# GpSimd normalises the attention probabilities; the transposed tile stays one PSUM tile

## The chip, the core and the metric

One core of one Trainium2 chip. The metric is the device time of one execution in microseconds (us), taken as the median of several runs. Two layers of a hybrid transformer backbone run as one program.

## The reference, cut to what matters

The change lies in attention, which each layer computes once for the 512 latent tokens (768 keys), and layer 0 also for the 256 context tokens (256 keys). There are 8 query heads of 64 channels on 2 key/value heads.

```python
def attention(q, k, v):
    ...
    def one_block(qi):
        s = jnp.einsum('bqhgd,bshd->bhgqs', qi, k).astype(jnp.float32)
        p = jax.nn.softmax(s, axis=-1).astype(v.dtype)
        return jnp.einsum('bhgqs,bshd->bqhgd', p, v)
    ...

def reference(...):
    for i in range(DEPTH):
        last = i == DEPTH - 1
        ...
        yx = mixer_out(qx, k_all, v_all, ux[..., V_END:P_END], ux[..., P_END:C_END], ux[..., C_END:], lp)
        if not last:
            yc = mixer_out(qc, kc, vc, uc[..., V_END:P_END], uc[..., P_END:C_END], uc[..., C_END:], lp)
        ...
```

## The kernel before

The program is written by hand, one instruction list for each engine; each list runs in order, and semaphores order the lists against one another. A counter (`Tally`) gives every awaited step a name; `seen(name)` is the semaphore value that a waiter needs.

Float32 products are made of three reduced-precision ones, so every operand exists as a high and a low part. Weights come in slabs of 128x1024: the SP queue loads a slab, ScalarE rounds it to the high part (L893), and GpSimd subtracts to get the low part (`split_run`, L425), two instructions ahead in a ring of four. These splits are GpSimd's main work.

Attention is cut into **units** (`units`, L274). A unit is one query tile of 128 rows against 768 keys; in layer 0 each head has a fifth, short unit that packs the two context query tiles against 256 keys each, a tile of 128x512. Layer 0 has 40 units, layer 1 has 32. All engines walk over the units in a software pipeline; the order is written out by hand in each list:

- TensorE (L765): scores of unit u+1 into PSUM region A (two buffers), then the six transposes of unit u-1 into PSUM region B (L736; one buffer), then a share of the products with the values (L757).
- VectorE (L1580): maximum of unit u (L1585) and its negative, scaled (L1589); for unit u-1 the reciprocal of the row sums (L1596) and the **normalisation**, the probabilities times that reciprocal in place (L1599); for unit u-2 the low part of the transposed tile, read from B (L1605). The last one frees B.
- ScalarE (L1067): exponential of unit u with its row sums (L1075), which frees A; then the high part of the transposed tile of unit u-1, read from B (L1086).

The transposes of a unit wait for its normalisation (`normed`) and for B to be free (`free`, `pt`). The probabilities have two buffers (`pr`, `probs` in the profile), and the exponential of unit u waits for the transposes of unit u-2.

GpSimd has no part in attention. Its list (L480) goes from the splits ahead of attention straight on to those behind it. The slabs of a layer are numbered; S_CONV is 8, RING is 4, so slab 12 is the last that GpSimd splits before attention ends: ScalarE rounds slab 13 only behind its own attention loop, at `result_of(s0 + S_CONV + 2)` (L1100).

Of the kernel before, what the change touches and what calls it, by code (L numbers as in the profile page):

```python
# [28 lines left out]
ALU = mybir.AluOpType  # L29
# [19 lines left out]
RING = 4  # L49
# [11 lines left out]
SLABS = _s  # L61
# [59 lines left out]
def build(nc, io, known):  # L121
# [22 lines left out]
    def seen(*name):  # L144


        if name not in known:
            assert not known, name
            return tallies["rounded"].sem, 1
        tally, value = known[name]  # L150
        return tallies[tally].sem, value
# [3 lines left out]
    with ctx:  # L155
# [107 lines left out]
        def lo_of(ly):  # L263

            return 0 if ly == 0 else CTX
# [8 lines left out]
        def units(ly):  # L274


            out, b = [], 0
            for h in range(HEADS):
                for q0, nq, nk in ([(CTX, 2, T), (CTX + 2 * P, 2, T)] + ([(0, 1, CTX)] if ly == 0 else [])):
                    out += [(h, q0, nk, q, nq, b) for q in range(nq)]  # L280
                    b += 1
            return out
# [23 lines left out]
        def q_tiles(unit):  # L306

            return 2 if unit[2] == CTX else 1
# [109 lines left out]
        @block.gpsimd  # L418
        def _(pool):

            def split_run(a, b):
                for s in range(a, b):
                    n = P * (slab_blocks(s % SLABS) if s >= RING else KT)
                    pool.wait_ge(rounded.sem, s + 1)
                    nc.gpsimd.tensor_tensor(wl[:, s % RING, 0:n], raw[:, s % RAW, 0:n], wh[:, s % RING, 0:n],  # L425
                                            ALU.subtract).then_inc(split, 1)

            def add_squares(ly, st, lo, k):
                pool.wait_ge(*seen("sq", ly, st, k))
                pool.wait_ge(*seen("sq", ly, st, k - 1))  # L430
                nc.gpsimd.tensor_tensor(square(k - 1)[:, lo:T], square(k - 1)[:, lo:T], square(k)[:, lo:T],
                                        ALU.add).then_inc(*pool_norm.up("sq2", ly, st, k - 1))

            def x_times(ly, st, lo, j):

                x_old = xm if st == "post1" else x
                if st == "post1":
                    pool.wait_ge(x_loaded[j], 16 * (ly + 2))
                pool.wait_ge(*seen("gy", ly, st, j))
                if j >= 2:  # L440
                    pool.wait_ge(*seen("vadd", ly, st, j - 2))
                out = xgy[:, j % 2, lo:T] if j else xgy_sum[:, lo:T]
                nc.gpsimd.tensor_tensor(out, x_old[:, j, lo:T], acc[:, j, lo:T], ALU.mult).then_inc(
                    *pool_norm.up("xgy", ly, st, j))

            def add_x(ly, st, lo, k):

                pool.wait_ge(*seen("rt", ly, st, k))
                nc.gpsimd.tensor_tensor(x[:, k, lo:T], x[:, k, lo:T], acc[:, k, lo:T], ALU.add).then_inc(
                    *pool_norm.up("x", ly, st, k))  # L450

            def ff_lows():

                pool.wait_ge(*seen("stat", 0, "pre2"))
                pool.wait_ge(*seen("fh", "shift"))
                nc.gpsimd.tensor_tensor(fl[:, :, 0:2], mod[:, 0, 3 * KT:4 * KT, :], fh[:, :, 0:2],
                                        ALU.subtract).then_inc(*pool_norm.up("fl", "shift"))
                for k in range(KT):
                    pool.wait_ge(*seen("fh", k))
                    nc.gpsimd.tensor_tensor(fl[:, k, 2:2 + T], ns[:, k, :], fh[:, k, 2:2 + T],  # L460
                                            ALU.subtract).then_inc(*pool_norm.up("fl", k))

            def lows(ly, st, lo):

                for k in lows_of(ly, st):
                    t = norm_tile(k) if (ly, st) == (0, "pre1") else scaled_tile(k)
                    pool.wait_ge(*seen("hh", ly, st, k))
                    nc.gpsimd.tensor_tensor(hl[:, k, lo:T], t[:, lo:T], hh[:, k, lo:T],
                                            ALU.subtract).then_inc(*pool_norm.up("hl", ly, st, k))
                    if (ly, st) == (1, "pre1") and k in (0, 2):  # L470
                        add_x(0, "post2", 0, pool_adds[k // 2])


            split_run(0, 2)
            for k in range(1, KT, 2):
                add_squares(0, "pre1", 0, k)
            split_run(2, RING)
            lows(0, "pre1", 0)
            at_s = RING
            for ly in range(LAYERS):  # L480
                lo = lo_of(ly)
                for j in range(KT):
                    stop = ly * SLABS + S_OUT + j + RING
                    split_run(at_s, stop)
                    at_s = stop
                    if j < KT - 1:
                        x_times(ly, "post1", lo, j)
                if ly == 0:
                    ff_lows()
                else:  # L490
                    lows(1, "pre2", lo)
                if ly == 0:
                    for j in range(KT):
                        stop = FF_OUT[2] + j + RING
                        split_run(at_s, stop)
                        at_s = stop
                        if j < KT - 1:
                            x_times(ly, "post2", lo, j)
                    split_run(at_s, SLABS + RING)
                    at_s = SLABS + RING  # L500
                    lows(1, "pre1", 0)
                else:
                    split_run(at_s, LAYERS * SLABS)
                    for k in pool_last:
                        add_x(ly, "post2", lo, k)
# [780 lines left out]
        def _(dve):  # L1286
            v = nc.vector

            def link(ins, tally, *name):

                ins.then_inc(*tally.up(*name))
                dve.wait_ge(*tally.ago())
# [229 lines left out]
            for ly in range(LAYERS):  # L1522
# [57 lines left out]
                for u in range(len(us) + 2):  # L1580
# [11 lines left out]
                    if 1 <= u <= len(us):  # L1592
                        h, q0, nk, q, nq, b = us[u - 1]
                        n, c = q_tiles(us[u - 1]), 2 * ((u - 1) % 8)
                        dve.wait_ge(*seen("free", "scores", ly, u - 1))
                        link(v.reciprocal(ust[:, 3, c:c + n], ust[:, 2, c:c + n]), dve_tmp)  # L1596
                        for r in range(n):
                            p_r = pr[:, (u - 1) % 2, r * nk:(r + 1) * nk]
                            v.tensor_scalar(p_r, p_r, ust[:, 3, c + r:c + r + 1], None, ALU.mult).then_inc(  # L1599
                                *(dve_tmp.up("normed", ly, u - 1) if r == n - 1 else dve_tmp.up()))  # L1600
                    if u >= 2:
                        h, q0, nk, q, nq, b = us[u - 2]
                        dve.wait_ge(*seen("pth", ly, u - 2))
# [375 lines left out]
```

## Time and profile before

| | |
|---|---|
| median of 3 runs | 2241.17 us (2239.71 to 2244.13) |
| the profiled execution: time, span | 2242.06 us, 2240.3 us |
| busy, of the span | TensorE 95%, VectorE 60%, ScalarE 35%, GpSimd 35% |
| VectorE's multiplies (L1599) | 80, median 0.62 us each |
| attention, from the first maximum to the last subtraction | 157.7 to 272.7 us (layer 0), 1426.2 to 1518.8 us (layer 1) |

The profile is one execution. Its rows name the engine (PE is TensorE, PEld its weight loads, DVE is VectorE, ACT is ScalarE, POOL is GpSimd), the line of the kernel, what is written and what is read, and, in brackets, how long the engine had stood idle and which instruction ended that. The first instruction with such a bracket is where a wait ended. Matmuls are pipelined, so a group's time runs from its first start to its last end.

### The profile page before, as it was taken

Reading aid. Unit: us, or ns where it says so; the run is one execution under the profiler, and the core shown is the slowest. Engines: PE = TensorE matmul, PEld = TensorE weight load, DVE = VectorE, ACT = ScalarE, POOL = GpSimd, SP = SyncE. Lnnn points to the kernel's source line nnn. Section 1 sums busy time; section 2 is a strip of 40 time slices with the busy share of each in tenths; the row PEclk is TensorE's granted clock in tenths of the full one; section 3 lists DMA queues with packets and bytes.
Section 4 is the critical chain, followed back from the end, with each engine's and each line's share of the span. In section 5 each row is a group of like instructions: output and inputs, shape, how many; then the busy total and the mean of one; then the engine's idle time right before and its main releaser. Section 6 shows DMA issues by size and latency. Waiting matters only on the chain.

```text
span 2240.3 us, 27947 instructions
## 1 busy us (share of the span) xinstructions
PE 2134.7 (95%) x11302; PEld 1807.4 (81%) x11302; DVE 1337.7 (60%) x1812; ACT 794.9 (35%) x1154; POOL 783.3 (35%) x359
## 2 busy tenths in 40 slices
PE   6889899999999999999999987899999999999997
PEld 6777788888888888888888876677867877888885
DVE  6459899856774587847616674798954353101113
ACT  2446711142324522223212344572234344222223
POOL 3220023232334433423323345103444555444442
PEclk9999999999999999999999989999999999999998
DMA  7110012123344134534323221102222332323321
GB/s 295 38 47 1 1 52 70 43 88 112 105 159 151 58 119 134 187 101 135 105 85 111 94 95 66 48 1 66 88 78 90 108 123 82 97 94 95 94 85 66
DMA packets 63200, 205.24 MB, mean 92 GB/s; under 512 B 7136, under 2 KB 8288, under 8 KB 62816
## 3 DMA queue, kind: packets, MB, share of 16 engines
q1 hardware_dynamic: 57744, 190.87, 26.2%
q10 hardware_dynamic: 5328, 12.59, 1.5%
q8 instruction: 90, 1.47, 0.3%
q14 instruction: 38, 0.31, 0.0%
HBM read 197.79 MB, written 5.64 MB: 91 GB/s over the span
## 4 chain that ended last, share of the span: by engine, by line
PE 78%; DVE 17%; ACT 2%; issue 1%; DMA 1%; POOL 1%; ACTq 0%; DVEq 0%
PE ps L529 70%; DVE conv_acc L1624 3%; DVE ps L1624 2%; DVE unit_stats L1585 2%; PE ps L555 2%; DVE pt1l L1605 1%; DVE probs L1599 1%; DVE pt0l L1605 1%; PE ps L736 1%; PE ps L592 1%; PE ps L573 1%; PE ps L613 1%; PE ps L583 1%; PE ps L757 1%; PE ps L600 1%
## 5 line engine op out<-in xcount | busy, mean ns | idle before, releaser
L425 POOL TENSOR_TENSOR w_l<-w_raw,w_h 128x1024 fp32r<-128x1024 f32 (+3 forms) x296 | 683.7, 2314 | 1305.7 <-ACT w_h L893 1305.4
L529 PE MATMUL ps<-h_h,w_h 128*128 128x512 f32 (+1 forms) x1296 | 430.4, 372 | 5.9 <-ACT t L1145 4.2
L529 PE MATMUL ps<-h_l,w_h 128*128 128x512 f32 (+1 forms) x1296 | 426.1, 369 | 0.0
L529 PE MATMUL ps<-h_h,w_l 128*128 128x512 f32 (+1 forms) x1296 | 425.3, 368 | 0.0
L893 ACT ACTIVATE w_h<-w_raw 128x1024 fp32r<-128x1024 f32 (+3 forms) x296 | 280.5, 950 | 212.2 <-PE ps L529 148.6
L529 PEld LDWEIGHTS ps<-h_h,w_h 128*128 128x128 f32 x1296 | 244.8, 190 | 55.8 <-ACT t L1145 6.6
L529 PEld LDWEIGHTS ps<-h_h,w_l 128*128 128x128 f32 x1296 | 245.7, 190 | 43.6
L529 PEld LDWEIGHTS ps<-h_l,w_h 128*128 128x128 f32 x1296 | 245.4, 189 | 42.9 <-issue 1.2
L1485 DVE CUSTOM_DVE_ANT_0 ps<-ada_raw,c_row 128x1024 f32<-128x1024 f32 x160 | 268.4, 1677 | 9.1 <-DMA ada_raw<-in_ada 4.1
L529 PE MATMUL ps<-f_h,w_h 128*128 128x258 f32 (+1 forms) x672 | 173.1, 339 | 0.9 <-DVE t L1810 0.9
L529 PE MATMUL ps<-f_h,w_l 128*128 128x258 f32 (+1 forms) x672 | 173.5, 340 | 0.0
L529 PE MATMUL ps<-f_l,w_h 128*128 128x258 f32 (+1 forms) x672 | 172.4, 338 | 0.0
L529 PE MATMUL ps<-mid_h,w_l 128*128 128x512 f32 (+1 forms) x528 | 160.7, 359 | 0.0
L529 PE MATMUL ps<-mid_h,w_h 128*128 128x512 f32 (+1 forms) x528 | 160.0, 357 | 0.1
L529 PE MATMUL ps<-mid_l,w_h 128*128 128x512 f32 (+1 forms) x528 | 159.1, 355 | 0.0
L1624 DVE SCALAR_TENSOR_TENSOR ps<-conv_in,vec,ps 128x512 f32<-128x512 f32 (+1 forms) x180 | 143.8, 845 | 2.1
L529 PEld LDWEIGHTS ps<-f_h,w_h 128*128 128x128 f32 x672 | 127.5, 190 | 16.1 <-DVE t L1810 1.2
L529 PEld LDWEIGHTS ps<-f_l,w_h 128*128 128x128 f32 x672 | 127.1, 189 | 14.6
L529 PEld LDWEIGHTS ps<-f_h,w_l 128*128 128x128 f32 x672 | 127.0, 189 | 14.6
L529 PEld LDWEIGHTS ps<-mid_h,w_h 128*128 128x128 f32 x528 | 99.4, 188 | 16.2 <-DVE acc L1835 0.4
L529 PEld LDWEIGHTS ps<-mid_l,w_h 128*128 128x128 f32 x528 | 99.2, 188 | 15.5
L529 PEld LDWEIGHTS ps<-mid_h,w_l 128*128 128x128 f32 x528 | 99.2, 188 | 14.7
(236 smaller groups left out, 3222.6 us busy)
## 6 DMA issues: line engine op xcount, KB each, us to landing
w_raw<-in_w SPq DMA_DIRECT2D x222, 512.0 KB, 3.6
ada_raw<-in_ada SPq DMA_DIRECT2D x80, 512.0 KB, 3.6
w_raw<-in_w SPq DMA_DIRECT2D x50, 256.0 KB, 3.2
ada_first<-in_ada SPq DMA_DIRECT2D x16, 512.0 KB, 6.7
w_raw<-in_w SPq DMA_DIRECT2D x16, 384.0 KB, 3.1
x<-in_x ACTq DMA_DIRECT2D x8, 384.0 KB, 17.6
x_again<-in_x ACTq DMA_DIRECT2D x8, 384.0 KB, 7.7
x_between<-x SPq DMA_DIRECT2D x8, 384.0 KB, 2.3
```

The costliest lines, as they stand in the source:

```text
L425: nc.gpsimd.tensor_tensor(wl[:, s % RING, 0:n], raw[:, s % RAW, 0:n], wh[:, s % RING, 0:n], ALU.subtract).then_inc(split, 1)
L529: ins = nc.tensor.matmul(at(out, c0, c1), w[:, s % RING, b * P:(b + 1) * P], m[:, kt, first + c0:first + c1], start=(kt == 0 and n == 0), ...
L555: ins = nc.tensor.matmul(at(out, c0, c1), w[:, s % RING, b * P:(b + 1) * P], m[:, k, first + c0:first + c1], start=(i == 0 and n == 0), st ...
L573: ins = nc.tensor.matmul(DD[:, 2 * k:2 * k + 2], ada_first[:, n % ADA_SLOTS, b * P:(b + 1) * P], silu_c[:, b, :], start=(b == 0), stop=(b ...
L583: ins = nc.tensor.matmul(at(B if w == "B" else OD, c0, c1), mat, src(c0, c1), start=True, stop=True)
L592: ins = nc.tensor.matmul(token_sum(kind, TOK[kind] + t, 1), src[:, t * P:(t + 1) * P], ones[:, 0:1], start=start and first, stop=stop and ...
L600: ins = nc.tensor.matmul(token_sum("q", c, 2), src[:, t * P:(t + 1) * P], blk[:, 0:P:HD], start=True, stop=True)
L893: nc.scalar.activation(wh[:, n % RING, 0:nb * P], raw[:, n % RAW, 0:nb * P], ACT.Copy).then_inc(*rounded.up())
L1485: link(v.tensor_tensor_reduce(out=scratch, in0=tile, in1=c_row[:, s, :], scale=1.0, scalar=0.0, op0=ALU.mult, op1=ALU.add, accum_out=mod[: ...
L1585: link(v.reduce_max(ust[:, 0, c:c + n], at(A[u % 2], 0, n * nk).rearrange("p (r k) -> p r k", k=nk), AX.X), dve_tmp)
L1605: v.tensor_tensor(key_rows(pl, us[u - 2]), by_key_tile(at(B, 0, nk * q_tiles(us[u - 2])), us[u - 2]), key_rows(ph, us[u - 2]), ALU.subtrac ...
L1624: return v.scalar_tensor_tensor(out=taps_of(ly, j), in0=src, scalar=w, in1=taps_of(ly, j), op0=ALU.mult, op1=ALU.add)
```

## The change

For each unit VectorE keeps the reciprocal and signals it (`recip`). The multiply by it, in place in the same buffer, goes to GpSimd, in a new loop `probabilities`. It waits for `recip` of the unit and signals `normed` from a counter of GpSimd. Ahead of that loop stands a `split_run` up to slab 12, so that the multiplies of a layer lie between the split of slab 12 and that of slab 13. The transposed tile is one piece in B as before, with one transpose group, one high and one low part for each unit. TensorE's and ScalarE's lists are as before.

```diff
@@ -471,6 +471,16 @@
+            def probabilities(ly):
+
+                for u, (h, q0, nk, q, nq, b) in enumerate(units(ly)):
+                    n, c = q_tiles((h, q0, nk, q, nq, b)), 2 * (u % 8)
+                    pool.wait_ge(*seen("recip", ly, u))
+                    for r in range(n):
+                        p_r = pr[:, u % 2, r * nk:(r + 1) * nk]
+                        nc.gpsimd.tensor_scalar(p_r, p_r, ust[:, 3, c + r:c + r + 1], None, ALU.mult).then_inc(
+                            *(pool_norm.up("normed", ly, u) if r == n - 1 else pool_norm.up()))
@@ -479,6 +489,9 @@
             for ly in range(LAYERS):
                 lo = lo_of(ly)
+                split_run(at_s, ly * SLABS + S_CONV + 1 + RING)
+                at_s = ly * SLABS + S_CONV + 1 + RING
+                probabilities(ly)
                 for j in range(KT):
@@ -1593,11 +1606,7 @@
                         dve.wait_ge(*seen("free", "scores", ly, u - 1))
-                        link(v.reciprocal(ust[:, 3, c:c + n], ust[:, 2, c:c + n]), dve_tmp)
-                        for r in range(n):
-                            p_r = pr[:, (u - 1) % 2, r * nk:(r + 1) * nk]
-                            v.tensor_scalar(p_r, p_r, ust[:, 3, c + r:c + r + 1], None, ALU.mult).then_inc(
-                                *(dve_tmp.up("normed", ly, u - 1) if r == n - 1 else dve_tmp.up()))
+                        v.reciprocal(ust[:, 3, c:c + n], ust[:, 2, c:c + n]).then_inc(*dve_tmp.up("recip", ly, u - 1))
```

VectorE, inside a head of layer 0, before: from the subtraction of a long unit over the maximum of the short unit (128x2) to the next subtraction but one.

```order
L1605 TENSOR_TENSOR pt0l<-ps,pt0h 128x6x128 [waits act_hi]
L1585 TENSOR_REDUCE unit_stats<-ps 128x2 [waits pe_done]
L1589 SCALAR_TENSOR_TENSOR unit_stats<-unit_stats,token_rs 128x2 [waits dve_tmp]
L1596 RECIPROCAL unit_stats<-unit_stats 128x1 [waits act_out]
L1599 TENSOR_SCALAR probs<-probs,unit_stats 128x768 [waits dve_tmp]
L1605 TENSOR_TENSOR pt0l<-ps,pt0h 128x6x128 [waits act_hi]
L1585 TENSOR_REDUCE unit_stats<-ps 128x1 [waits pe_done]
L1589 SCALAR_TENSOR_TENSOR unit_stats<-unit_stats,token_rs 128x1 [waits dve_tmp]
L1596 RECIPROCAL unit_stats<-unit_stats 128x2 [waits act_out]
L1599 TENSOR_SCALAR probs<-probs,unit_stats 128x256 [waits dve_tmp]
L1599 TENSOR_SCALAR probs<-probs,unit_stats 128x256
L1605 TENSOR_TENSOR pt0l<-ps,pt0h 128x6x128 [waits act_hi]
```

The same place after the change; its lines are numbered 9 or 13 higher.

```order
L1614 TENSOR_TENSOR pt0l<-ps,pt0h 128x6x128 [waits act_hi]
L1598 TENSOR_REDUCE unit_stats<-ps 128x2 [waits pe_done]
L1602 SCALAR_TENSOR_TENSOR unit_stats<-unit_stats,token_rs 128x2 [waits dve_tmp]
L1609 RECIPROCAL unit_stats<-unit_stats 128x1 [waits act_out]
L1614 TENSOR_TENSOR pt0l<-ps,pt0h 128x6x128 [waits act_hi]
L1598 TENSOR_REDUCE unit_stats<-ps 128x1 [waits pe_done]
L1602 SCALAR_TENSOR_TENSOR unit_stats<-unit_stats,token_rs 128x1 [waits dve_tmp]
L1609 RECIPROCAL unit_stats<-unit_stats 128x2 [waits act_out]
L1614 TENSOR_TENSOR pt0l<-ps,pt0h 128x6x128 [waits act_hi]
```

The multiplies and their wait on the reciprocal are gone; the subtraction follows the reciprocal directly.

GpSimd, around the start of attention in layer 0, before.

```order
L468 TENSOR_TENSOR h_l<-norm_tmp,h_h 128x768 [waits act_hi] x3
L425 TENSOR_TENSOR w_l<-w_raw,w_h 128x1024 [waits rounded] x13
L425 TENSOR_TENSOR w_l<-w_raw,w_h 128x512 [waits rounded]
L425 TENSOR_TENSOR w_l<-w_raw,w_h 128x1024 [waits rounded]
L425 TENSOR_TENSOR w_l<-w_raw,w_h 128x512 [waits rounded]
```

And after (one head of the eight; the other seven repeat the last three rows).

```order
L468 TENSOR_TENSOR h_l<-norm_tmp,h_h 128x768 [waits act_hi] x3
L425 TENSOR_TENSOR w_l<-w_raw,w_h 128x1024 [waits rounded] x9
L481 TENSOR_SCALAR probs<-probs,unit_stats 128x768 [waits dve_tmp] x4
L481 TENSOR_SCALAR probs<-probs,unit_stats 128x256 [waits dve_tmp]
L481 TENSOR_SCALAR probs<-probs,unit_stats 128x256
```

Of the 13 splits in a row nine now stand ahead of the multiplies and four behind them.

## Rows read from the trace of the kernel before

**Rows 1.** The page's chain of waits, shares of the span by engine.

```profile
PE 78%; DVE 17%; ACT 2%; issue 1%; DMA 1%; POOL 1%; ACTq 0%; DVEq 0%
```

**Rows 2.** Windows: span; busy us (count) of PE, PEld, DVE, ACT, POOL; clock; DMA.

```profile
182.76:264.15 81.39, 74.15 (x542) 62.53 (x541) 76.97 (x157) 59.65 (x121) 0.00 (x0) 1.00 0.01 1
1443.00:1506.73 63.73, 60.59 (x439) 50.63 (x438) 62.11 (x116) 45.49 (x82) 0.00 (x0) 1.00 0.00 1
```

**Rows 3.** Timeline, layer 1: start us, us, engine, line, operation, out<-in, count, [idle before <-releaser].

```profile
1443.00 0.96 DVE L1605 TENSOR_TENSOR pt1l<-ps,pt1h 128x768 fp32r<-128x768 f32 x1
...
1443.93 0.96 DVE L1585 TENSOR_REDUCE unit_stats<-ps 128x1 f32<-128x768 f32 x1
...
1444.01 0.64 PEld L736 LDWEIGHTS ps<-const,probs 128*128 128x128 f32 x6 [0.56 <-DVE pt1l L1605]
...
1444.01 0.87 PE L736 MATMUL ps<-const,probs 128*128 128x128 f32 x6
...
1444.92 0.16 DVE L1589 SCALAR_TENSOR_TENSOR unit_stats<-unit_stats,token_rs 128x1 f32<-128x1 f32 x1
...
1444.92 0.81 ACT L1086 ACTIVATE pt1h<-ps 128x768 fp32r<-128x768 f32 x1 [0.73 <-PE ps L736]
...
1445.00 0.16 DVE L1596 RECIPROCAL unit_stats<-unit_stats 128x1 f32<-128x1 f32 x1
...
1445.19 0.62 DVE L1599 TENSOR_SCALAR probs<-probs,unit_stats 128x768 f32<-128x768 f32 x1
...
1445.77 0.96 DVE L1605 TENSOR_TENSOR pt1l<-ps,pt1h 128x768 fp32r<-128x768 f32 x1
...
1445.79 0.87 PE L726 MATMUL ps<-k_split,q_split 128*128 128x256 f32 x4
...
1446.69 0.96 DVE L1585 TENSOR_REDUCE unit_stats<-ps 128x1 f32<-128x768 f32 x1
```

**Rows 4.** Timeline, layer 0, around the short unit of a head.

```profile
188.31 0.96 DVE L1605 TENSOR_TENSOR pt0l<-ps,pt0h 128x768 fp32r<-128x768 f32 x1
...
189.32 0.66 PE L736 MATMUL ps<-const,probs 128*128 128x128 f32 x4 [0.15 <-DVE pt0l L1605]
...
190.01 0.60 ACT L1086 ACTIVATE pt0h<-ps 128x512 fp32r<-128x512 f32 x1 [0.77 <-PE ps L736]
...
190.46 0.62 DVE L1599 TENSOR_SCALAR probs<-probs,unit_stats 128x768 f32<-128x768 f32 x1
...
191.00 0.68 DVE L1605 TENSOR_TENSOR pt0l<-ps,pt0h 128x512 fp32r<-128x512 f32 x1
...
193.57 0.95 DVE L1605 TENSOR_TENSOR pt1l<-ps,pt1h 128x768 fp32r<-128x768 f32 x1
```

**Rows 5.** Timeline, the first unit of each layer's attention loop.

```profile
161.25 0.16 DVE L1596 RECIPROCAL unit_stats<-unit_stats 128x1 f32<-128x1 f32 x1 [0.17 <-ACT probs L1075]
...
162.30 0.22 PEld L736 LDWEIGHTS ps<-const,probs 128*128 128x128 f32 x1
...
1429.10 0.17 DVE L1596 RECIPROCAL unit_stats<-unit_stats 128x1 f32<-128x1 f32 x1 [0.17 <-ACT probs L1075]
...
1430.07 0.85 PE L736 MATMUL ps<-const,probs 128*128 128x128 f32 x6
```

**Rows 6.** GpSimd's two-input instruction: timeline, and mean by form (last row).

```profile
1348.86 0.94 DVE L1371 TENSOR_TENSOR acc<-acc,ps 128x768 f32<-128x768 f32 x1
...
1349.88 1.83 POOL L449 TENSOR_TENSOR x<-x,acc 128x768 f32<-128x768 f32 x1 [0.28 <-DVE acc L1371]
...
L449 POOL TENSOR_TENSOR x<-x,acc 128x512 f32<-128x512 f32 x4 | 5.1, 1264 | 23.1 <-DVE acc L1371 23.1
```

**Rows 7.** Timeline, layer 0, VectorE beside a running GpSimd instruction.

```profile
157.65 2.36 POOL L425 TENSOR_TENSOR w_l<-w_raw,w_h 128x1024 fp32r<-128x1024 f32 x1 [0.73 <-ACT w_h L893]
...
157.68 0.96 DVE L1585 TENSOR_REDUCE unit_stats<-ps 128x1 f32<-128x768 f32 x1
...
158.67 1.35 DVE L1589 SCALAR_TENSOR_TENSOR unit_stats<-unit_stats,token_rs 128x1 f32<-128x1 f32 x1
```

## Prediction

> **What bounds the kernel now.** I read the page's chain of waits first: TensorE is 78% of it, VectorE 17% [rows 1], so a VectorE instruction is worth something only where TensorE waits for VectorE. The change touches one stage, attention, which the kernel passes twice: 40 units in layer 0, 32 in layer 1. The windows over its steady part come next [rows 2]. The granted clock is 1.00 (2.4 GHz). Layer 1: 116 VectorE instructions at five a unit are 23 units in 63.73 us, **2.77 us a unit**. Layer 0: six heads, from the first subtraction of one to that of the sixth after it, take 81.39 us, 13.57 us for a head's five units. GpSimd does nothing there. TensorE (60.59 us busy) and VectorE (62.11) look equally full, so busy time does not name the bound; the order of events does.
>
> The timeline of one unit says what 2.77 us is made of [rows 3]. PSUM region B holds one transposed tile. VectorE subtracts it (L1605, starting 1443.00, 0.96); 0.05 later TensorE transposes the next (1444.01, 0.87, after an idle 0.56 that the subtraction ended); 0.04 later ScalarE copies it (1444.92, 0.81); 0.04 later VectorE subtracts again (1445.77). 0.96 + 0.05 + 0.87 + 0.04 + 0.81 + 0.04 = 2.77 us. I call it the B ring. It closes exactly on the measured period, and **the normalisation is not in it**. VectorE's own sequence is nearly as long: the normalisation runs from 1445.19 to 1445.81 and overlaps the start of the next subtraction, with some 0.05 us to spare. Two limits lie on top of each other; taking work from one leaves the other.
>
> In layer 0 the fifth unit of a head is short (two query tiles of 256 keys, a 128x512 tile). Its ring is shorter, and there VectorE is the later one [rows 4]: the copy of the short tile ends at 190.61, but the subtraction starts at 191.00, behind the normalisation that began at 190.46. From 188.31 over 191.00 to 193.57 the two steps take 5.26 us. The ring alone would need 0.96 + 0.05 + 0.66 + 0.03 + 0.60 + 0.03 = 2.33 for the step to the short tile, and 0.68 + 0.05 + 0.87 + 0.04 + 0.81 + 0.04 = 2.49 for the step back: 4.82.
>
> **What the change removes.** The multiplies on VectorE: one of 0.62 us for each long unit [rows 3], two half-size ones for a short unit, 72 slots of 0.54 us because the next instruction overlaps (190.46 to 191.00, [rows 4]). In layer 1 the freed time is worth nothing: the B ring still takes 2.77. In layer 0 at most 5.26 - 4.82 = 0.44 us for each of the 7 places where a short unit stands between two long ones: 3.1 us in all. That is the ceiling of the gain, 0.14% of the span.
>
> **What it adds.** The same multiplies on GpSimd, X us for a long unit, and two handovers. VectorE to GpSimd took 0.08 (1348.86 + 0.94 to 1349.88, [rows 6]); GpSimd to TensorE I take as the same, so 0.15 for both. No GpSimd multiply by a scalar is in this trace. From below X is bounded by VectorE's 0.62 for the same tile. From above by GpSimd's two-input instruction on a tile of this size, 1.83 [rows 6]. A gain from X below 0.62 would change nothing, since the ring is then the later one in any case. Between the ends: 512 elements took 1.26 and 768 took 1.83, so 2.2 ns an element and 0.15 fixed. The two-input form moves three streams, the multiply two; two thirds of 1.68 plus 0.15 is 1.27. I take **X = 1.3**, an estimate, and keep both ends. A short unit's two multiplies of 256 elements come by the same reckoning to 2 x (0.15 + 0.37) = 1.04, less than X, and are nowhere the later ones.
>
> **The wait that it adds.** Transpose of unit u+2 now follows this path from transpose of unit u, through program order on TensorE and VectorE: transposes and values until the next scores start (1444.01 to 1445.79, 1.78), scores 0.87 and handover 0.03 (reduction starts 1446.69), the reduction to the reciprocal 1.07 (0.99 + 0.08), the reciprocal 0.16, 0.15 handovers and X [rows 3, 4]. That is 4.06 + X for two units, against 5.54 from two turns of the B ring. **The break-even is X = 1.48.** Below it, layer 1 keeps its 2.77. At the short unit of layer 0 the ring gives 4.82, so there the path rules from X = 0.76 on: 4.06 + 1.3 = 5.36, 0.10 more than today's 5.26; break-even 1.20.
>
> In front of each loop nothing hides the multiply, since the first transpose waits for it. Layer 1: reciprocal at 1429.10 + 0.17 + 0.15 + 1.3 = 1430.72, where the transpose began at 1430.07: 0.6 late. Layer 0: 161.25 + 0.16 + 0.15 + 1.3 = 162.86 against a weight load at 162.30: 0.6 late [rows 5]. X enters these two places in full. At the end of each loop the last units run on the ring, and nothing changes.
>
> GpSimd's queue: the weight splits of slabs up to 12 stand ahead of the multiplies, the split of slab 13 behind all of them. ScalarE rounds slab 13 only after attention, so no split comes later; GpSimd is idle in between [rows 2], and X of 1.3 to 1.83 fits in 2.77. SP's queue is not touched. Cost: nothing.
>
> **A port.** VectorE's tiny negmax at 158.67 took 1.35 us instead of 0.16, and ended with the GpSimd instruction that had started at 157.65 and took 2.36; the reduction before it, which reads PSUM, ran its usual 0.96 under the same instruction [rows 7]. So here a GpSimd instruction held up a VectorE one with two SBUF inputs, and spared one that reads PSUM, as the subtraction also does with one of its inputs. In the new loop one such instruction per unit remains, the negmax. It starts 0.08 before the reciprocal that releases the multiply, so the multiply has 2.77 - 0.08 - 0.16 - 0.08 = 2.45 us until the next negmax. It collides only from X = 2.45.
>
> **The sum.** Layer 0: 7 x 0.10 = 0.7, its start 0.6. Layer 1: 0 and 0.6. Together +1.9 us on the profiled execution's own 2242.06 us: 2244.0. That execution lies 0.9 above the median of the runs, so on the scale of the medians **2243 us**.
>
> **Rivals.**
> A, *slower: GpSimd becomes the late one.* Mechanism and place as above, deciding from X = 1.48 on in both layers. At X = 1.83: layer 1 pays (4.06 + 1.83 - 5.54) = 0.35 for two units, 15.5 times: 5.4. Layer 0's head becomes 5.89 + 5.89 + 2.77 = 14.55 instead of 13.57, seven times: 6.9. The two starts: 2 x (0.6 + 0.53) = 2.3. Sum +14.6: 2256.7, or 2256 by the medians. The 4.5 us that count as slower are reached at X = 1.51 (3.5 us at 1.48, and some 31 us for each us of X beyond). For it: every large GpSimd row is a two-input one at 1.83. Against: the multiply reads one stream less. The Trainium skill (GPSIMD Engine Reference, Performance versus the Vector engine) speaks for a middle: it measures some 1.8 cycles an element for a tight loop, an estimate of 1.15 us for 768 elements at its 1.2 GHz, and the sum by it would be 2242; for the two-input form it gives about 2.6 cycles, which the trace's 2.2 ns an element bears out.
> B, *GpSimd runs at VectorE's pace.* X = 0.62: 7 x -0.44 = -3.1, starts -0.2: -3.3, 2238.8, or 2238 by the medians, which still counts as no change. The Trainium skill (GPSIMD Engine Reference, Engine selection) calls a one-input elementwise operation "roughly line-rate" on GpSimd; by that this rival is the result. No row here shows a one-input form, so I give it a fair chance and not the most.
> C, *faster: VectorE is the bound in attention.* For it: 17% of the chain of waits is VectorE's [rows 1], and it is busy 62.11 of 63.73 us [rows 2]. Were it so, each unit would lose its 0.54 slot: 72 x 0.54 = 39 us, 2203. Against it stands the ring, which closes to 0.01 us with a wait of TensorE on the subtraction in every unit.
> D, *it does not do what it says.* The order of the instructions shows the multiplies gone from VectorE and standing on GpSimd, so this is excluded.
>
> **How the numbers follow.** The forecast case, X from 0.9 to 1.5, gets 0.46; B, X below 0.9, 0.18; A 0.31; C and anything that gains beyond the ceiling 0.05. A difference of 0.2% (4.5 us) is about the least that a measurement of this kernel can tell from no change. B and the forecast case both stay inside it: same 0.64, slower 0.31, faster 0.05. The range goes from rival B's end to just beyond A's at X = 1.83: 2237.5 to 2257.
>
> **What the new profile would show.** The GpSimd rows of the multiply give X directly; everything else follows from it. Right: the subtractions of layer 1 still 2.77 apart, VectorE idle some 0.5 a unit, the transposes still waiting for the subtraction; in layer 0 a head at 13.1 to 13.7. Wrong: transposes released by GpSimd in layer 1 (X over 1.48, rival A), a negmax longer than 0.16 inside the loop, a period under 2.77 (rival C), or a second stretch of lower clock behind the later start of layer 0, which this sum holds at nothing.

## The result, and the profile after

The changed kernel takes 2271.97 us (median of four runs, 2270.04 to 2275.16) against 2240.44 for the kernel before on the same chip (four runs, 2239.43 to 2244.13). The ratio is 1.0139, with a 95% interval of 1.0122 to 1.0157: slower by 31.5 us, where 2243 was forecast and 2257 was the end of the range. The profiled execution spans 2269.0 us, 28.7 more than the one before.

The page's first section, and its chain of waits by engine (the line that answers [rows 1]):

```profile
PE 2134.7 (94%) x11302; PEld 1807.8 (80%) x11302; DVE 1299.2 (57%) x1732; ACT 795.1 (35%) x1154; POOL 940.7 (41%) x439
...
PE 76%; DVE 14%; POOL 4%; ACT 3%; issue 2%; DMA 1%; ACTq 0%; DVEq 0%; SPq 0%
```

GpSimd now holds 4% of the chain, where it had 1%. VectorE fell from 60% busy to 57%, and that bought nothing. The groups of GpSimd's new line, long and short units apart (busy, mean ns of one | idle time before and what ended it):

```profile
L481 POOL TENSOR_SCALAR probs<-probs,unit_stats 128x768 f32<-128x768 f32 x64 | 141.2, 2207 | 60.0 <-DVE unit_stats L1609 60.0
L481 POOL TENSOR_SCALAR probs<-probs,unit_stats 128x256 f32<-128x256 f32 x16 | 14.6, 927 | 12.7 <-DVE unit_stats L1609 12.7
```

**The multiply takes 2.21 us.** The prediction took 1.3, between 0.62 and 1.83. It is slower than the two-input instruction of the same size [rows 6], which was to be its upper bound. All 64 take between 2.20 and 2.21, whatever VectorE does beside them, so no collision with VectorE makes them long.

The same two windows as [rows 2], with the same columns:

```profile
182.76:264.15 81.39, 63.69 (x470) 53.99 (x468) 53.22 (x107) 52.44 (x106) 56.52 (x32) 1.00 0.00 1
1443.00:1506.73 63.73, 52.40 (x343) 44.20 (x343) 39.88 (x77) 36.51 (x64) 43.09 (x20) 0.89 0.01 3
```

In layer 1's window TensorE issues 343 matmuls where it issued 439, and in layer 0's 470 where it issued 542. The list of waits of 180 to 280 (us in total, times, longest) says on whom it waits, with GpSimd in turn waiting for the reciprocal:

```profile
POOL probs L481 <- DVE unit_stats L1609: 31.5, 34, 1.6
PE ps L749 <- POOL probs L481: 20.4, 27, 1.5
```

And the timeline of layer 1, the place that answers [rows 3], is one closed path over two units:

```profile
1488.96 2.21 POOL L481 TENSOR_SCALAR probs<-probs,unit_stats 128x768 f32<-128x768 f32 x1 [1.14 <-DVE unit_stats L1609]
...
1491.32 0.84 PE L749 MATMUL ps<-const,probs 128*128 128x128 f32 x6 [0.73 <-POOL probs L481]
...
1493.04 0.87 PE L739 MATMUL ps<-k_split,q_split 128*128 128x256 f32 x4
...
1493.94 0.96 DVE L1598 TENSOR_REDUCE unit_stats<-ps 128x1 f32<-128x768 f32 x1
...
1495.02 0.15 DVE L1609 RECIPROCAL unit_stats<-unit_stats 128x1 f32<-128x1 f32 x1
...
1495.26 2.21 POOL L481 TENSOR_SCALAR probs<-probs,unit_stats 128x768 f32<-128x768 f32 x1 [1.11 <-DVE unit_stats L1609]
```

The path runs so: the multiply of unit u (2.21), 0.15 to TensorE, transposes and values of unit u up to the scores of unit u+3 (1.72), their maximum starting 0.90 later, the reciprocal of unit u+2 1.08 after that (0.15), and 0.09 to GpSimd: 6.30 us, with the multiply of unit u+1 in between at 1491.94. The subtractions (L1614) stand 3.31 and 3.00 apart by turns, 6.31 for two units, where the B ring needed 5.54. The bracket behind the transposes names GpSimd, as the prediction said it would if X were over 1.48.

**Where the 28.7 us lie.** Layer 0's first subtraction comes 0.7 later than before, and its loop, from first to last subtraction, takes 120.55 us instead of 106.94 (+13.6). In layer 1 the first subtraction comes 7.91 us behind the first maximum instead of 5.74 (+2.2), and the loop takes 99.54 instead of 85.89 (+13.65). The stretch between the two loops is 1.6 shorter. Sum 28.5.

### The profile page after: what moved, and what is told of

It is laid out like the page before. It is cut to its first block, busy times and chain, and to the rows that moved or that the text cites. A ratio compares the mean times of both kernels' runs of the same rounds, so it can differ in the third digit from the quotient of the medians.

```text
span 2269.0 us, 27947 instructions
## 1 busy us (share of the span) xinstructions
PE 2134.7 (94%) x11302; PEld 1807.8 (80%) x11302; DVE 1299.2 (57%) x1732; ACT 795.1 (35%) x1154; POOL 940.7 (41%) x439
## 3 DMA queue, kind: packets, MB, share of 16 engines
q8 instruction: 90, 1.47, 0.3%
## 4 chain that ended last, share of the span: by engine, by line
PE 76%; DVE 14%; POOL 4%; ACT 3%; issue 2%; DMA 1%; ACTq 0%; DVEq 0%; SPq 0%
PE ps L542 69%; POOL probs L481 3%; DVE conv_acc L1633 3%; DVE ps L1633 2%; PE ps L749 2%; PE ps L568 2%; DVE unit_stats L1598 1%; PE ps L586 1%; DVE pt1l L1614 1%; PE ps L605 1%; ACT pt1h L1099 1%; DMA w_raw<-in_w 1%; PE ps L596 1%; DVE pt0l L1614 1%; PE ps L626 1%
## 5 line engine op out<-in xcount | busy, mean ns | idle before, releaser
L481 POOL TENSOR_SCALAR probs<-probs,unit_stats 128x768 f32<-128x768 f32 (+1 forms) x80 | 155.8, 1951 | 72.7 <-DVE unit_stats L1609 72.7
```

Source lines behind the costliest of these rows:

```text
L481: nc.gpsimd.tensor_scalar(p_r, p_r, ust[:, 3, c + r:c + r + 1], None, ALU.mult).then_inc(*(pool_norm.up("normed", ly, u) if r == n - 1 els ...
```

## The experiments

All ratios are to the kernel before on the same chip, with their 95% interval. X is GpSimd's time for one multiply of a long unit.

### Is it X? The same multiply over fewer columns

Two kernels are the changed one with the multiply cut to its first 8 columns, and to half of its columns.

```diff
-                        p_r = pr[:, u % 2, r * nk:(r + 1) * nk]
+                        p_r = pr[:, u % 2, r * nk:r * nk + 8]
```

> The changed kernel, but GpSimd multiplies only the first 8 columns of each tile (the rest stays unnormalised); both handovers and all waits stay. Theory (the length X of the multiply is the whole cost): X near 0.3 us, the B ring rules everywhere, subtractions of layer 1 2.77 us apart, a head of layer 0 at 13.1; about 4 us under the kernel before: 2236 to 2238. Rival (the handovers between engines, or GpSimd and VectorE blocking each other, make the cost): it stays at 2255 or more.

```diff
-                        p_r = pr[:, u % 2, r * nk:(r + 1) * nk]
+                        p_r = pr[:, u % 2, r * nk:r * nk + nk // 2]
```

> The changed kernel with the multiply on the first half of the columns (384 of 768; the rest stays unnormalised). From 0.93 us for 256 and 2.21 us for 768 columns X should be 1.25, under the break-even of 1.48: 2.77 a unit in layer 1, a head of 13.6 in layer 0, both starts 0.5 late: 2241 to 2243, no difference from the kernel before. If cost grows in proportion to the length instead of setting in at a break-even, half of the loss stays: 2256.

The groups of the multiply, of the first kernel and then of the second:

```profile
L481 POOL TENSOR_SCALAR probs<-probs,unit_stats 128x8 f32<-128x8 f32 x80 | 24.3, 306 | 172.7 <-DVE unit_stats L1609 172.7
```

```profile
L481 POOL TENSOR_SCALAR probs<-probs,unit_stats 128x384 f32<-128x384 f32 x64 | 79.6, 1244 | 95.8 <-DVE unit_stats L1609 95.8
```

Times: 2242.81 us at X = 0.31, ratio 0.9999 (0.9985 to 1.0013), and 2247.61 at X = 1.24, ratio 1.0018 (1.0003 to 1.0032). In both, layer 1's subtractions are 2.77 apart once the loop is under way: **X makes the lengthening of the steady loop**, and the new semaphores and handovers cost it nothing. The second time is a miss all the same: 2241 to 2243 was expected, no difference, and it is 4 us (1 to 7) slower. Its first units of layer 1 are late (see the clock, below). At X = 1.24 the two steps around a short unit of layer 0 take 2.34 + 3.02 = 5.36 us, where the path gives 4.06 + 1.24 = 5.30. At X = 0.31 they take 2.34 + 2.63 = 4.97, not the 4.82 that the prediction took as the ring's floor. That shrinks the possible gain, and the first kernel does not reach the 2236 to 2238 that I expected of it; its first units in both layers ran at 3.43 us instead of 2.77 (see the clock, below).

### What sets X? Other forms of the same instruction

The two-input form, which reads the reciprocal as a broadcast operand:

```diff
-                        nc.gpsimd.tensor_scalar(p_r, p_r, ust[:, 3, c + r:c + r + 1], None, ALU.mult).then_inc(
+                        nc.gpsimd.tensor_tensor(p_r, p_r, ust[:, 3, c + r:c + r + 1].to_broadcast([P, nk]), ALU.mult).then_inc(
```

> The multiply as a two-input GpSimd instruction, the reciprocal broadcast along the row by its access pattern. If the two-input form costs 1.83 us as it does elsewhere in this kernel, layer 1 takes (4.06 + 1.83) / 2 = 2.95 a unit and the time falls by 16 us to 2256. If the broadcast operand or this place in the loop makes any GpSimd instruction take 2.2, the time stays at 2272.

And the scalar form with a constant in place of the operand:

```diff
-                        nc.gpsimd.tensor_scalar(p_r, p_r, ust[:, 3, c + r:c + r + 1], None, ALU.mult).then_inc(
+                        nc.gpsimd.tensor_scalar(p_r, p_r, 0.5, None, ALU.mult).then_inc(
```

> The changed kernel with the constant 0.5 in place of the reciprocal as the multiplier (output not the reference's), to measure the instruction: if reading the per-row scalar is what makes it 2.21 us, it falls to 1.3 or below and the time to some 2243; if the loop over the elements is, it stays at 2.2 and the time at 2272.

The groups of the multiply, of the one and then of the other:

```profile
L481 POOL TENSOR_TENSOR probs<-probs,unit_stats 128x768 f32<-128x768 f32 x64 | 93.9, 1467 | 86.5 <-DVE unit_stats L1609 86.5
```

```profile
L481 POOL TENSOR_SCALAR probs<-probs 128x768 f32<-128x768 f32 x64 | 136.4, 2132 | 62.7 <-DVE unit_stats L1609 62.6
```

I had expected 1.83 of the two-input form, and it takes **1.47**. The kernel takes 2249.79 us, ratio 1.0035 (1.0021 to 1.0048), so naming another instruction gets back three quarters of the loss. It also lands on the predicted break-even: 4.06 + 1.47 = 5.53 against the ring's 5.54, and the subtractions of layer 1 are 2.78 apart. The prediction's sum at that X was some 3.5 us; measured are 8, and about 2 of the difference are three first units of layer 1 at 3.44, 3.44 and 3.57 us. The constant changes X only from 2.21 to 2.13 (2268.23 us in one run), so it is the scalar form that is slow here, not the reading of its operand. Why that form is slow, no run shows. The period follows: 4.06 + 2.13 = 6.19 for two units, and 3.11 measured for one.

### Does the wait path decide? The reciprocal ahead of the maximum

With X left at 2.21, the reciprocal of unit u-1 is put ahead of the maximum of unit u on VectorE. That takes the scores and the maximum out of the path.

```diff
                 for u in range(len(us) + 2):
+                    if 1 <= u <= len(us):
+                        ...
+                        dve.wait_ge(*seen("free", "scores", ly, u - 1))
+                        v.reciprocal(ust[:, 3, c:c + n], ust[:, 2, c:c + n]).then_inc(*dve_tmp.up("recip", ly, u - 1))
                     if u < len(us):
...
-                    if 1 <= u <= len(us):
-                        ...
-                        dve.wait_ge(*seen("free", "scores", ly, u - 1))
-                        v.reciprocal(ust[:, 3, c:c + n], ust[:, 2, c:c + n]).then_inc(*dve_tmp.up("recip", ly, u - 1))
```

> The changed kernel with one step moved: VectorE takes the reciprocal of unit u-1 ahead of the maximum of unit u, not behind it. The multiply still takes 2.21 us. Theory (what costs is the wait path, which runs through the maximum): the multiply starts some 0.9 us sooner, the path through three units becomes 7.6 us against 8.3 for the B ring, the ring rules again at 2.77 a unit: 2240 to 2245. Rival (a GpSimd multiply of 2.2 us is too long for the loop wherever it stands): 2265 or more.

2254.17 us, ratio 1.0042 (1.0026 to 1.0058): 22 of the 31 us are back with X unchanged. So the path through program order was the cause, and X its largest term. It still misses the 2240 to 2245 expected. In layer 1 most subtractions are 2.76 to 2.80 apart, but six are 3.07 or 3.08. There the transposes are released by GpSimd: ScalarE's copy of a finished product (L1076, 0.38 us at 1459.05) stands ahead of the exponential, and multiply and transposes (1463.17) come late by it. In this trace the six make some 2 us, three first units at 3.43, 3.43 and 3.64 another 2, and the later first subtraction of layer 1 makes 2.8.

The multiply now overlaps VectorE's negmax (L1607 here), which reads two SBUF inputs. First a long unit, where the negmax is not held up, then a short one, where it is:

```profile
1486.02 2.21 POOL L481 TENSOR_SCALAR probs<-probs,unit_stats 128x768 f32<-128x768 f32 x1 [0.16 <-DVE unit_stats L1598]
...
1486.81 0.16 DVE L1607 SCALAR_TENSOR_TENSOR unit_stats<-unit_stats,token_rs 128x1 f32<-128x1 f32 x1
```

```profile
183.49 2.20 POOL L481 TENSOR_SCALAR probs<-probs,unit_stats 128x768 f32<-128x768 f32 x1 [0.82 <-DVE unit_stats L1598]
...
184.01 0.39 DVE L1607 SCALAR_TENSOR_TENSOR unit_stats<-unit_stats,token_rs 128x2 f32<-128x2 f32 x1
```

What differs is how far the multiply has come. The 55 negmaxes that run beside a long multiply in this trace and start 0.79 us or more behind its start take 0.16. The eight that start 0.53 behind it take 0.38 or 0.39 and end 0.91 behind it, 1.3 us before the multiply does. So the scalar form holds VectorE up as well, but only early in its run and not to its end.

### Would VectorE's time have been worth anything? No multiply at all

The kernel before without its multiplies, on any engine: rival C's question.

```diff
-                        link(v.reciprocal(ust[:, 3, c:c + n], ust[:, 2, c:c + n]), dve_tmp)
-                        for r in range(n):
-                            ...
+                        v.reciprocal(ust[:, 3, c:c + n], ust[:, 2, c:c + n]).then_inc(*dve_tmp.up("normed", ly, u - 1))
```

> The kernel before without any normalising multiply (output not the reference's); the transposes wait for the reciprocal only. It prices the freed VectorE time. B ring: layer 1 still 2.77 a unit, a head of layer 0 at 13.3, 2236 to 2239. If VectorE is the bound in attention: 0.54 for each of 72 units, 2203.

2241.51 us, ratio 0.9982 (0.9970 to 0.9994): some 4 us, where rival C needed 39. Two subtractions of layer 1 in a row:

```profile
1476.53 0.96 DVE L1601 TENSOR_TENSOR pt0l<-ps,pt0h 128x768 fp32r<-128x768 f32 x1 [0.65 <-ACT pt0h L1086]
...
1479.30 0.96 DVE L1601 TENSOR_TENSOR pt0l<-ps,pt0h 128x768 fp32r<-128x768 f32 x1 [0.65 <-ACT pt0h L1086]
```

Still 2.77 apart, and VectorE now waits 0.65 for ScalarE's copy. **The freed time turns into idle time of VectorE.** This is the B ring, seen with nothing on top of it, and it bounds what any move of the multiply can bring in this schedule.

### Opening the B ring

The ring exists because the transposed tile has one piece and one buffer. With the tile in two pieces of 256 and 512 columns (transposes, copy and subtraction in two parts, each with its own semaphore) TensorE can refill the first piece while VectorE reads the second. The core of that edit, on TensorE:

```diff
-                    for k in range(nk * q_tiles(us[u]) // P):
-                        ins = nc.tensor.transpose(at(B, k * P, (k + 1) * P), pr[:, u % 2, k * P:(k + 1) * P], ident)
-                    ins.then_inc(*pe_done.up("pt", ly, u))
+                    for i, (k0, k1) in enumerate(((0, 2), (2, nk * q_tiles(us[u]) // P))):
+                        if u:
+                            pe.wait_ge(*seen("low", ly, u - 1, i))
+                        for k in range(k0, k1):
+                            ins = nc.tensor.transpose(at(B, k * P, (k + 1) * P), pr[:, u % 2, k * P:(k + 1) * P], ident)
+                        ins.then_inc(*pe_done.up("ptp", ly, u, i))
```

First with everything so far: two pieces, early reciprocal, two-input multiply.

> The B tile in two pieces (256 and 512 columns; transposes, high and low part for each piece, each piece freed by itself), the reciprocal ahead of the maximum, and the multiply on GpSimd as a two-input instruction of 1.47 us. With the ring cut, exponential, reciprocal, maximum, negmax, exponential (2.45 us) is the longest cycle: 2.5 a unit, 19 us faster than the kernel before, 2222. If TensorE or VectorE's order hold it at 2.77: 2241.

2251.42 us, ratio 1.0029 (1.0017 to 1.0040): 6 us slower than the kernel before, where 19 us faster was expected. The steady period is 2.87. Its timeline, layer 1:

```profile
1485.73 1.47 POOL L487 TENSOR_TENSOR probs<-probs,unit_stats 128x768 f32<-128x768 f32 x1 [1.41 <-DVE unit_stats L1612]
...
1486.54 0.67 DVE L1621 SCALAR_TENSOR_TENSOR unit_stats<-unit_stats,token_rs 128x1 f32<-128x1 f32 x1
...
1487.25 0.99 ACT L1100 ACTIVATE probs<-ps,unit_stats,token_rs 128x768 f32<-128x768 f32 x1 [0.23 <-DVE unit_stats L1621]
```

The negmax takes 0.67 instead of 0.16 and ends at 1487.21, as the GpSimd instruction does (1485.73 + 1.47 = 1487.20). This is the collision of [rows 7], now in every unit, and the exponential waits behind it (L1100, 0.23 here). The negmax starts 0.81 us behind the multiply here, as it did with the scalar form (0.79), and is held to the end, where it had not been held at all. To test that, the next two kernels take the cause away: the maximum is written to unused columns of PSUM region A, so that the negmax has one SBUF input left.

```diff
-                        link(v.reduce_max(ust[:, 0, c:c + n],
+                        top = A[u % 2][:, 128:128 + n]
+                        link(v.reduce_max(top,
...
-                        v.scalar_tensor_tensor(out=ust[:, 1, c:c + n], in0=ust[:, 0, c:c + n], scalar=-1.0,
+                        v.scalar_tensor_tensor(out=ust[:, 1, c:c + n], in0=top, scalar=-1.0,
```

> As split_early_tt, but VectorE writes the maximum to unused columns of PSUM region A, so that the negmax has one SBUF input instead of two. In split_early_tt the negmax took 0.67 us in place of 0.16, ending with the GpSimd multiply that ran beside it, in a period of 2.87. Theory (GpSimd's two-input instruction holds up a VectorE instruction with two SBUF inputs): the negmax falls to 0.16, the period to 2.36 to 2.5, 20 us or more faster than the kernel before. If the stall has another cause, the negmax stays at 0.67 and the time at +6 us.

> The same without the split: the tile in one piece, the reciprocal early, the 1.47 us multiply, the maximum in PSUM. B ring theory: no path is longer than the ring any more, so 2.77 a unit in layer 1 and a head at 13.3 in layer 0, where it stops: 2 us faster to 1 us slower than the kernel before. If the ring is not a limit of its own: some 2.5 a unit, 20 us faster.

The first of them, two pieces included, takes **2217.59 us, ratio 0.9888 (0.9866 to 0.9910)**, and beats both kernels of this case. The second, with the tile in one piece, takes 2240.25, ratio 0.9982 (0.9970 to 0.9994), some 4 us faster than the kernel before and a little more than the 2 expected at most. The timeline and a window of the first, layer 1 (columns as in [rows 2]):

```profile
1484.69 1.47 POOL L487 TENSOR_TENSOR probs<-probs,unit_stats 128x768 f32<-128x768 f32 x1 [1.20 <-DVE unit_stats L1612]
...
1485.51 0.16 DVE L1622 SCALAR_TENSOR_TENSOR unit_stats<-ps,token_rs 128x1 f32<-128x1 f32 x1
```

```profile
1450.00:1500.00 50.00, 49.10 (x375) 44.38 (x373) 39.08 (x91) 41.07 (x86) 26.41 (x18) 1.00 0.01 1
```

The negmax is back at 0.16 in the middle of the GpSimd instruction. From 1433.65 to 1487.95 the subtractions take 2.47 a unit, and TensorE is busy 49.10 of 50 us. In the kernel with one piece the same window stays on the ring:

```profile
1450.00:1500.00 50.00, 47.50 (x346) 39.70 (x345) 38.58 (x72) 36.28 (x64) 26.43 (x19) 1.00 0.01 1
```

2.77 a unit, whatever is taken from VectorE. And the two pieces alone, on the kernel before and on the changed one:

> The kernel before with only the B tile in two pieces; VectorE normalises. The ring is cut, but VectorE's own sequence of 2.66 us, with one instruction more, stays: 2.70 to 2.77 a unit, between 5 us faster and no difference.

> The changed kernel with only the B tile in two pieces; the multiply of 2.21 us, the reciprocal behind the maximum. The path through scores, maximum and multiply does not pass the pieces: 3.1 a unit as before the split, 25 to 31 us slower than the kernel before. If one piece was what cost the time: no slower than the kernel before.

On the kernel before: 2235.52 us, ratio 0.9961 (0.9947 to 0.9974), 2.72 a unit in layer 1. The window and three rows of its timeline:

```profile
1450.00:1500.00 50.00, 48.38 (x350) 39.99 (x349) 48.74 (x111) 39.21 (x84) 0.00 (x0) 1.00 0.01 1
```

```profile
1481.50 0.60 ACT L1099 ACTIVATE pt1h<-ps 128x512 fp32r<-128x512 f32 x1 [0.29 <-PE ps L747]
...
1481.92 0.62 DVE L1613 TENSOR_SCALAR probs<-probs,unit_stats 128x768 f32<-128x768 f32 x1
...
1482.45 1.02 DVE L1620 TENSOR_TENSOR pt1l<-ps,pt1h 128x256 fp32r<-128x256 f32 x2
```

VectorE is busy 48.74 of 50 us, but in the kernel before it is busy 48.73 in the same window, so the busy time does not tell. The order does: ScalarE's copy of the second piece has ended at 1482.10, and the two subtractions start at 1482.45, behind the multiply. With the ring open VectorE's own sequence is the bound, which it was not before. The time is 9 us (6 to 12) shorter, where 5 was expected at most. The steps in the steady loops, 0.05 in layer 1's 32 units and 13.18 instead of 13.57 us for a head of layer 0, make some 4 us. From the first maximum to the end of the last subtraction the traces show 109.1 us in place of 115.0 in layer 0 and 90.4 in place of 92.6 in layer 1, 8.1 in all, so the rest lies at the starts and ends of the loops; 1.3 of it are two units of layer 0 that the trace of the kernel before ran at the lower clock.

On the changed kernel: 2262.84, ratio 1.0090 (1.0068 to 1.0113). There the GpSimd path rules as before: the multiplies start at 1483.94, 1486.53 and 1490.18, 6.24 us for two units against 4.06 + 2.21 = 6.27. It is 20 us slower than the kernel before (15 to 25), less than the 25 to 31 expected.

So each limit alone is worth little: opening the ring some 0.4%, freeing VectorE some 0.2%, and both together 1.1% (with the two-input multiply, the early reciprocal and the maximum in PSUM). Moving the multiply pays more than some 4 us only with the ring open.

### The clock at the starts of the loops

The kernel before was profiled once more.

> The kernel before, profiled once more, to see whether the granted clock at the start of the attention loops is a property of the kernel or changes between executions. If of the kernel: 1.00 from 2 us after the first reciprocal of layer 1 on. If it changes: some units at 3.43 us at half the clock, at 0.66 us each.

2240.67 us in one run. Three-microsecond windows at the start of layer 1 (columns as in [rows 2], the clock is the third number from the end), first of this second trace of the kernel before, then of the changed kernel:

```profile
1422.00:1425.00 3.00, 2.67 (x8) 2.01 (x8) 1.65 (x2) 1.22 (x2) 2.50 (x2) 0.50 0.41 96
1425.00:1428.00 3.00, 1.33 (x6) 0.69 (x6) 2.55 (x6) 2.06 (x4) 0.66 (x1) 0.96 0.57 191
1428.00:1431.00 3.00, 1.68 (x12) 1.25 (x12) 2.93 (x6) 1.78 (x3) 0.00 (x0) 1.00 0.16 63
1431.00:1434.00 3.00, 1.81 (x15) 1.38 (x14) 2.90 (x6) 1.78 (x3) 0.00 (x0) 1.00 0.01 3
```

```profile
1437.00:1440.00 3.00, 2.82 (x8) 2.01 (x8) 1.79 (x3) 1.07 (x2) 2.49 (x2) 0.50 0.45 124
1440.00:1443.00 3.00, 1.08 (x5) 0.54 (x4) 1.93 (x5) 2.06 (x4) 1.49 (x2) 1.00 0.59 178
1443.00:1446.00 3.00, 1.63 (x8) 1.66 (x9) 0.98 (x3) 0.08 (x1) 3.00 (x2) 0.57 0.12 48
1446.00:1449.00 3.00, 2.39 (x11) 1.67 (x10) 2.06 (x4) 1.71 (x3) 0.46 (x2) 0.50 0.00 0
```

Both are at 0.50 (1.2 GHz) with the first scores and at full clock (2.4 GHz) behind them. Then the changed kernel's clock falls once more, up to 1457, behind a stretch in which TensorE was busy 1.08 of 3 us. At 0.50 six transposes take 1.51 us, where they had taken 0.85 [rows 5], and a turn of the B ring 3.43 instead of 2.77. The changed kernel's first three intervals in layer 1 are 3.43, 3.49 and 4.45.

In the four traces without a multiply on GpSimd (the kernel before twice, without the multiply, in two pieces) the clock is full by the first subtraction of layer 1's loop or within 1 us behind it. Of the ten with it, eight are still at 0.50 some us behind that subtraction, and six of these begin layer 1 with two or three intervals of 3.4 us or more; the two that read the maximum from PSUM are at full clock there. That speaks for a cost of the later start that the prediction left out. But the kernel with X = 0.31 is among the eight, with three units at 3.43, though its first transposes start only 0.5 us later behind the reciprocal than before. And in layer 0 the kernel before itself shows 2.77, 3.44, 3.44 at its start in one trace and 3.43, 3.43, 4.16 in the other. With one trace of most kernels this stays open. It is worth up to 3 us a start, a tenth of the loss.

The clock also bears on how far two single traces can be compared. The 25 runs of the kernel before beside the first experiments go from 2237.59 us at a mean granted clock of 0.984 to 2250.23 at 0.977. And the stretch between the two attention loops, where all the kernels compute the same, takes 1152 to 1160 us in the fourteen traces. So a difference of some us between two profiled spans says nothing by itself; the loops' own intervals and the medians do.

## Why the prediction was wrong

**What failed is one term, X.** The prediction put it so: "The two-input form moves three streams, the multiply two; two thirds of 1.68 plus 0.15 is 1.27", with 1.83 as the upper end, "From above by GpSimd's two-input instruction on a tile of this size". Both assume that GpSimd's time goes by operands read. The runs show 2.21 for the scalar form, 1.83 for two full inputs and 1.47 for one full and one broadcast input, on the same 128x768 tile. The one that reads least took longest. An instruction of another form is no bound for one that the trace does not show, and with a break-even at 1.48 inside the range of X the whole verdict hung on it.

The trace of the kernel before could have warned. Rival A says that "every large GpSimd row is a two-input one at 1.83", and that is misread. These are two-input rows on the same 128x768 tile, by form (busy, mean ns | idle before):

```profile
L468 POOL TENSOR_TENSOR h_l<-norm_tmp,h_h 128x768 fp32r<-128x768 f32 x11 | 21.6, 1975 | 37.7 <-ACT h_h L955 37.6
L460 POOL TENSOR_TENSOR f_l<-norm_tmp,f_h 128x768 fp32r<-128x768 f32 x8 | 13.5, 1692 | 7.0 <-ACT f_h L926 6.6
L431 POOL TENSOR_TENSOR norm_tmp<-norm_tmp 128x768 f32<-128x768 f32 x4 | 10.1, 2541 | 8.9 <-ACT norm_tmp L908 8.9
```

Single ones go from 1.54 to 2.79 us. So even the two-input form had no upper end at 1.83, and the measured 2.21 lies inside what the trace showed. What spreads those rows, no run shows. The Trainium skill (GPSIMD Engine Reference, Engine selection) calls a one-input elementwise operation roughly line-rate on GpSimd; by the 2.21 measured beside VectorE's 0.62 that does not hold here, and the rival that rested on it, B at 2238, lies 34 us below the result.

**What held.** With X = 2.21 put into the prediction's own formulas:

| place | formula | worked out | measured |
|---|---|---|---|
| layer 1, two units | 4.06 + X | 6.27 | 6.31 |
| layer 0, a head | 2 x (4.06 + X) + 2.77 | 15.31 | 15.40 |
| layer 1's loop | 15.5 x (6.27 - 5.54) | +11.3 | +13.65 |
| layer 0's loop | 7 x (15.31 - 13.57) | +12.2 | +13.6 |
| both starts | 2 x (0.6 + 0.91) | +3.0 | +2.9 |

The sum is +26.5, against +30.2 measured in the same places. That the starts agree is luck: the formula has 1.5 for each, and measured are 0.7 in layer 0 and 2.2 in layer 1. The handovers were put at 0.15 for both and took 0.09 and 0.15, hence 6.31 and not 6.27. The formulas for the steady periods also held at X = 1.24, 1.47 and 2.13, though the whole kernels at 1.24 and 1.47 came out some 3 and 4 us slower than the sum. So rival A had the mechanism, the place and the point from which it decides; only its price, at 1.83, was too low, and its chance, 0.31, as well.

**The B ring and the ceiling.** Right: without any multiply layer 1 stays at 2.77. Rival C falls with it. The ceiling of 3.1 us was a little high, because the two steps around the short unit have a floor of 4.97, not 4.82: 7 x 0.29 is 2.0.

**GpSimd's queue and the ends of the loops** cost nothing, as held: the stretch between the loops, where the weight splits follow, did not grow (it is 1.6 us shorter), and from layer 1's last subtraction to the end of the span the changed kernel takes 0.2 us more than the one before.

**The port.** The number was right: no negmax inside the loop is longer than 0.16 at X = 2.21, under the 2.45 given. The rule behind it, that a GpSimd instruction holds up a VectorE one with two SBUF inputs, held for both forms, but not in the same way: the two-input form holds it to its own end (1487.21 against 1487.20), the scalar form lets go early (184.40, where the multiply ends at 185.69). The Trainium skill (SBUF — State Buffer, Who interferes with whom) says that such a VectorE instruction contends with a GpSimd instruction that reads SBUF. The traces agree, and add that under the scalar form a negmax that starts 0.79 us in meets nothing.

**The clock at the starts** was held at nothing. In the trace after, the slow first units make an estimated 1.9 of the 2.3 us that layer 1's loop took beyond the formula: its first three intervals sum to 11.37 us, and three at the steady 3.155 to 9.47.

## What to carry to other kernels

Before moving an instruction to another engine, follow one item of work through the program order of every engine it passes until the path closes, and compare the time of that path with the period you have; the difference is what the moved instruction may cost. Here it was 1.48 us, and the instruction took 2.21. If the trace has no row of that very instruction form, measure it before anything is built on it, and look at all rows of that size and not at one: an instruction that does the same with another form took two thirds of the time. Where two limits lie on top of each other, taking one away brings little, and that says nothing about what both would bring.

## What the runs showed of the hardware

- GpSimd's multiply by a per-partition scalar, float32, in place: 0.31 us for 8 columns, 0.60 for 128, 0.93 for 256, 1.24 for 384, 2.21 for 768, which is 2.5 ns an element and 0.29 fixed. With a constant 2.13. The two-input form with a broadcast operand takes 0.61 for 256 and 1.47 for 768.
- VectorE's small instruction with two SBUF inputs waits for the end of a running two-input GpSimd instruction (0.67 instead of 0.16, and 1.35 in [rows 7]). Under a GpSimd multiply by a scalar (128x768, 2.21 us) it takes 0.38 when it starts 0.53 us behind the multiply (8 of 8) and 0.16 when it starts 0.79 or more behind it (55 of 55). With one of its inputs in PSUM it takes 0.16 under the two-input form, at 0.55 as at 0.82 us behind its start.
- GpSimd's two-input instructions on a 128x768 tile took from 1.54 to 2.79 us in one trace, 1.83 in the rows that the prediction went by.
- A handover took 0.09 us from VectorE to GpSimd and 0.15 from GpSimd to TensorE.
